# Four TensorE jobs of a decoder step moved into the next chunk, and a new order of the cross-attention jobs in chunk 47

## The reference

```python
h = rmsnorm(x, g_mix)
proj = h @ w_in                      # pool channels | q | k | v, 512 each
A = causal pooling of 4 channel groups, windows 2, 4, 8, 16, then a map per group
B = attention, 8 heads of 64, rotary  # prompt: causal; decode: 256 cached keys + own
x = x + concat(A, B) @ w_out
q = rmsnorm(x, g_cross) @ w_cq       # 4 heads of 256
p = softmax(q . mk / 16)             # 256 memory keys
x = x + (p @ mv) @ w_co
x = x + relu(rmsnorm(x, g_mlp) @ w_up)**2 @ w_down
y = rmsnorm(x, g_final)
```

## Time and profile before

| | us |
|---|---|
| median of 3 runs (lowest, highest) | 419.35 (419.28, 420.08) |
| the profiled execution, its own time | 421.09 |
| its span, first to last instruction | 419.1 |
| TensorE busy in the span | 412.7 (98%) |
| VectorE, ScalarE, GpSimd busy | 253.1, 227.0, 30.9 |

### The profile page before, as it was taken

The page is one execution under the profiler, slowest core; times in us unless marked ns, Lnnn a source line. Parts: engine busy times, 40 slices in busy tenths (PEclk is TensorE's granted clock), DMA queues, the critical chain, the costliest instruction groups (busy, mean ns, idle before and its releaser), DMA issues.

```text
span 419.1 us, 8425 instructions
## 1 busy us (share of the span) xinstructions
PE 412.7 (98%) x3372; PEld 386.7 (92%) x3372; DVE 253.1 (60%) x400; ACT 227.0 (54%) x392; POOL 30.9 (7%) x41
## 2 busy tenths in 40 slices
PE   9999999999999999999999999999999999999995
PEld 9998989986879998948899999999999999999995
DVE  4799989666355784633259777666667534454302
ACT  5876958725454664424267666566565433453313
POOL 1003026000000220000022000000000000010011
PEclk9999999999999999999999999999999999999999
DMA  8999858965988966989527646555565655545002
GB/s 288 384 386 359 283 194 251 349 253 191 404 295 317 386 218 226 370 309 335 218 102 248 205 141 199 185 187 163 184 200 196 196 172 192 183 158 185 2 2 103
DMA packets 37257, 96.60 MB, mean 230 GB/s; under 512 B 4186, under 2 KB 13274, under 8 KB 37082
## 3 DMA queue, kind: packets, MB, share of 16 engines
q1 hardware_dynamic: 35106, 92.24, 63.3%
q10 hardware_dynamic: 2112, 3.82, 2.5%
HBM read 91.73 MB, written 4.54 MB: 230 GB/s over the span
## 4 chain that ended last, share of the span: by engine, by line
PE 89%; DMA 5%; DVE 2%; SPq 1%; issue 1%; ACT 0%; DVEq 0%
PE psum L1104 75%; PE psum L826 4%; DMA raw<-in_w_in 2%; PE psum L1046 2%; PE psum L941 2%; DMA stage<-in_mem_v 2%; PE psum L954 1%; DMA pages<-in_page_table 1%; PE psum L838 1%; PE psum L878 1%; SPq L772 1%; PE psum L887 1%; PE psum L925 1%; PE psum L947 0%; DVE rstd L1586 0%
## 5 line engine op out<-in xcount | busy, mean ns | idle before, releaser
L1392 DVE TENSOR_TENSOR w_lo<-raw,w_hi 128x1024 fp32r<-128x1024 f32 x67 | 82.4, 1239 | 62.2 <-ACT w_hi L1124 62.0
L1124 ACT ACTIVATE w_hi<-raw 128x1024 fp32r<-128x1024 f32 (+1 forms) x73 | 74.0, 1021 | 60.7 <-PE psum L1104 45.4
L1104 PE MATMUL psum<-mix_hi,w_hi 128*128 128x264 f32 (+1 forms) x288 | 82.8, 287 | 0.0
L1104 PE MATMUL psum<-mix_lo,w_hi 128*128 128x264 f32 (+1 forms) x288 | 81.5, 283 | 0.0
L1104 PE MATMUL psum<-mix_hi,w_lo 128*128 128x264 f32 (+1 forms) x288 | 81.5, 283 | 0.0
L1104 PE MATMUL psum<-act_hi,w_hi 128*128 128x264 f32 x232 | 66.3, 286 | 0.0
L1104 PE MATMUL psum<-act_lo,w_hi 128*128 128x264 f32 x232 | 65.6, 283 | 0.0
L1104 PE MATMUL psum<-act_hi,w_lo 128*128 128x264 f32 x232 | 65.4, 282 | 0.0
L1104 PEld LDWEIGHTS psum<-mix_hi,w_hi 128*128 128x128 f32 x288 | 54.3, 188 | 0.9 <-issue 0.8
L1104 PEld LDWEIGHTS psum<-mix_lo,w_hi 128*128 128x128 f32 x288 | 54.3, 189 | 0.1
L1104 PEld LDWEIGHTS psum<-mix_hi,w_lo 128*128 128x128 f32 x288 | 54.3, 189 | 0.0
(11 more groups left out here) (208 smaller groups left out, 813.7 us busy)
## 6 DMA issues: line engine op xcount, KB each, us to landing
raw<-in_w_down SPq DMA_DIRECT2D x20, 512.0 KB, 3.3
raw<-in_w_up SPq DMA_DIRECT2D x18, 512.0 KB, 4.3
raw_more<-in_w_up SPq DMA_DIRECT2D x14, 512.0 KB, 3.7
stage<-in_mem_v SPq DMA_DIRECT2D x12, 512.0 KB, 6.5
raw_more<-in_w_down SPq DMA_DIRECT2D x12, 512.0 KB, 4.2
stage<-in_cache_v SPq DMA_DIRECT2D x16, 256.0 KB, 6.2
keysT<-in_cache_k SPq DMA_DIRECT2D x16, 256.0 KB, 5.0
keysT<-in_mem_k SPq DMA_DIRECT2D x8, 512.0 KB, 6.5
```

The lines of the kernel that those rows point to most:

```text
L1104: mm = pe.matmul(out, a, b, start=first and m == 0, stop=end_ and m == 2)
L1124: return nc.scalar.activation(out, in_, ACT.Copy, scale=scale)
L1392: V.tensor_tensor(lo_of(c), raw_of(c), hi_of(c).bitcast(F32), ALU.subtract).then_inc(w_lo_ready, 1)
```

## The change

The plan of jobs differs in chunk 47 alone. The table `LATER` names four places inside a chunk (chunk, tile); TensorE runs the jobs listed there behind that tile's matmuls. It leaves them out of its walk through `JOBS`. The other engines, the banks and the buffers still go by `JOBS` and `ORDER`, in which those jobs belong to the chunk before: `S` to 8, `P_T` to 14, `c_attn` to 31, `stat c` to 41.

```diff
-    put(47, ("xP_T", 1), ("xP_S", 2), ("xc_O", 0, 0), ("xP_O", 0), ("xS", 1, 0), ("xS", 1, 1), ("xc_O", 0, 1), ("xP_O", 1), ("xc_T", 1), ("xc_attn", 0), ("xP_S", 3), ("xP_T", 2))
+    put(47, ("xP_T", 1), ("xP_S", 2), ("xc_O", 0, 0), ("xP_O", 0), ("xS", 1, 0), ("xS", 1, 1), ("xP_O", 1), ("xc_O", 0, 1), ("xc_T", 1), ("xP_S", 3), ("xc_attn", 0), ("xP_T", 2))
...
 JOBS = plan_jobs()
+LATER = {
+    (9, 1): [('S', 0)],
+    (15, 0): [('P_T', 0), ('P_T', 1), ('P_T', 2)],
+    (32, 1): [('c_attn',)],
+    (42, 0): [('stat', 'c')],
+}
+LATE_JOBS = [j for late in LATER.values() for j in late]
...
                     if last_of_group and x < len(banks_of(g)) - 1:
                         mm.then_inc(bank_full[bank], 1)
+                    for job in LATER.get((c, x), ()):
+                        run(job)
...
                 for job in JOBS[c]:
-                    run(job)
+                    if job not in LATE_JOBS:
+                        run(job)
```

## The result

The change makes the kernel slower. The median of four runs is 423.92 us (423.13 to 424.45) against 419.58 (419.28 to 420.08), a ratio of 1.0100 with a 95% interval from 1.0085 to 1.0115. The forecast of 419.9 with a range of 418.9 to 420.7 was wrong. The profiled execution took 424.45 us, with a span of 422.4 us.

A forecast was written before the change was run, and what follows sets the result against it. TensorE, busy 412.7 of 419.1 us, was taken to bound the kernel. The moves' -0.28 and chunk 47's +0.83 gave +0.55, which with the median of 419.35 made 419.9 us, range 418.9 to 420.7.

The forecast's parts named there:

- So 2.34 us of TensorE's time is in reach.: Waits the change could remove: 0.83 us at the head scores (`kT`), 1.51 at the second cross output's value tile.
- The moves, -0.28: Sum up to chunk 47: -0.83 at the scores, +0.05 at P_T, +0.45 at S 4, +0.05 for leaving a chunk.
- The waits at P_T and S 4: P_T in chunk 15 loses 0.05 (0 to 0.3); S 4 waits 0.45 (0.2 to 0.75) for its bank.
- a tie by the sum: P_T, moved behind one tile of chunk 15, comes at 53.45; the normalised heads it needs finish at 53.43.
- one of the prediction's own signs of being wrong: A wait at P_T over 0.3 us was listed among what would show the forecast wrong.
- The idle time of VectorE for `w_hi`: Before S 4: 0.35 us idle on VectorE, released by chunk 14's end through ScalarE, was to go.
- The held `w_lo`: Before S 4: GpSimd's addition holds VectorE's second `w_lo` about 0.7 us, bank free at 57.5, wait 0.45.
- `c_attn` and `stat c`: Moves into chunks 32 and 42: TensorE waited at neither, so nothing is gained; no new wait expected.
- Chunk 47, +0.83, bounds 0.5 and 1.2: New order removes the 1.51 us tile wait, but chunk 48 waits for xc_attn 0's low part: net cost 0.83.
- the gain of 1.51 at the value tile: Chunk 47: xP_O 1 ahead of xc_O 0 1 covers the tile's landing, so its 1.51 us wait is gone.
- the softmax chain: xP_S 3's softmax precedes xc_attn 0's low part: 3.0 us from xP_S 3's last issue until chunk 48 can start.
- the clock, put at nothing: Before chunk 48: TensorE idle some 2.2 us; the sum held no term for a lower clock.

The follow-up runs named there:

- e10: The kernel before, no edit, profiled a second time: span 417.7 us, chunk 46 to 48 in 23.11 us.
- e11: The kernel before, no edit, profiled a third time: span 417.0 us, chunk 46 to 48 in 22.61 us.
- e1: The kernel before with the four moved jobs alone, chunk 47 in its old order: 419.58 us against 419.93, ratio 0.9987.
- e4: The changed kernel with the four transposes of xP_T 2 done six times to fill the idle time: 421.93 us against 419.93 before, ratio 1.0056.
- e6: The four moves, with chunk 47's list ending xP_T 2, xc_attn 0, xP_S 3: 419.52 us against 419.79 for the kernel before, ratio 0.9998.
- e2: The kernel before with the new order of chunk 47 alone, no moved job: 424.18 us against 419.93, ratio 1.0096.
- e5: The changed kernel, xc_attn 0 back ahead of xP_S 3 on ScalarE and VectorE, TensorE's order kept: 420.08 us against 419.79 before, ratio 1.0005.
- e7: The changed kernel again, no edit, in a second set of runs: 423.48 us against 419.79 for the kernel before, ratio 1.0080.
- e9: The changed kernel with the transposes of xP_T 2 done three times: 422.03 us against 420.12 for the kernel before, ratio 1.0047.

## Why the prediction was wrong

**"So 2.34 us of TensorE's time is in reach."** Wrong in size. Both waits vary from execution to execution. The tile wait was 1.51 in the shown profile and 0 to 0.78 in four others; the scores start 0.95 behind the last matmul in the shown profile and 0.21 to 0.73 in e10 and e11. A normal step is 0.12, so 0.09 to 0.61 was to be had there. The shown profile's own time, 421.09, was 1.74 above the median of 419.35 that the prediction names beside it (1.0 to 1.5 above the medians of later sets), and part of what I read as the kernel's waits was that execution's. The prediction added its terms to the median as if both were the same execution.

**The moves, -0.28.** Not contradicted: e1 is at -0.35 (-1.2 to +0.1), an interval that holds zero. The waits at P_T and S 4 appeared where they were placed in the changed kernel's profile, but they are no fixed price of the moves: e1, e4 and e6 have the moves and show neither, and e2 has no moves and shows 0.5 for `uext`. Chunk 3 to 16 takes 46.84 to 47.67 in the five profiles without moves and 46.72 to 48.02 in the seven with all four. In the changed kernel's profile they cost more than the gain, +0.57 up to chunk 16, since `kT` ended at 34.26 there and not at 33.71, later than in any other profile, and all of VectorE's work behind it with it. Its rows with TensorE's at the same places:

```profile
33.12 1.14 DVE L1488 TENSOR_TENSOR kT<-kT,crossed 128x528 f32<-128x528 f32 x1
...
52.14 1.83 DVE L1579 TENSOR_TENSOR soft<-soft,stats 128x512 f32<-128x512 f32 x2
...
57.94 0.76 DVE L1443 TENSOR_TENSOR uext<-psum,rstd 128x264 f32<-128x264 f32 x2
```

```profile
34.50 1.59 PE L845 MATMUL psum<-kT,qT 32*128 32x128 f32 x32
...
54.11 1.17 PE L885 MATMUL psum<-const,soft 128*128 128x128 f32 x9 [0.37 <-DVE soft L1579]
...
58.50 0.73 PE L845 MATMUL psum<-kT,qT 32*128 32x128 f32 x16 [0.72 <-DVE uext L1443]
```

P_T stood at a tie by the sum (53.45 against 53.43), and 0.5 us of lateness on VectorE became 0.53 of wait, in full; over 0.3 there was one of the prediction's own signs of being wrong. The idle time of VectorE for `w_hi`, which should have gone with an earlier chunk 14, was also still there: in this execution ScalarE waited for the weights' landing, not for TensorE.

```profile
54.42 1.06 ACT L1134 ACTIVATE w_hi<-raw 128x1024 fp32r<-128x1024 f32 x1 [0.80 <-DMA raw<-in_w_ck]
```

The held `w_lo` did not come about. GpSimd's addition starts at 55.86, 0.35 behind the start of the second `w_lo` and not ahead of it, as in the kernel before (55.26 against 54.91), and that `w_lo` takes 1.22. So S 4's wait came from the lateness alone. The term was also summed wrongly: a bank free 0.43 earlier (57.29) and then held for 0.7 is free at 57.99, which gives a wait of 0.9 and not 0.45.

**`c_attn` and `stat c`.** Right: no wait, and 16 to 46 is 106.77 in both kernels.

**Chunk 47, +0.83, bounds 0.5 and 1.2.** The mechanism was right (e5), the size was not. Chunk 46 to 48 takes 25.33 or 25.34 in all five executions with this order. Against the shown profile that is +1.19, since chunk 48 started 3.24 us behind xP_S 3's last issue (191.56 to 194.80) and not 3.0, and xP_S 3 itself came 0.12 later in the frame of chunk 46. The 2.87 up to the end of the scalings were met exactly (191.56 to 194.43); the small low part and the signal took 0.37 and not 0.15. But against the old order as it usually runs (22.61 to 23.41) it is +1.9 to +2.7: the tile wait that the new order takes away is mostly not there. Without that wait the old order needs 22.62 and the new one 2.71 more: 2.44 in front of chunk 48 (2.80 from the last transposes to its start, against 0.36) and 0.27 in the steps before.

**The step that failed, part one: the gain of 1.51 at the value tile,** set against the softmax chain in the term +0.83. It was one execution's wait, 0 to 0.78 in four others, so the term, bounded by 0.5 and 1.2, came out at +1.9 to +2.7.

**Part two: the clock, put at nothing.** The forecast said that TensorE would stand idle for some 2.2 us, and it did, 2.20; nothing in the sum gave that idle time an effect behind its end, and no reason was given. Chunk 48's first matmul to chunk 49's takes 6.88 where the clock fell and 5.31 to 5.43 in all that kept it, 1.56 for each fall. It fell in eleven of sixteen executions, and with the twenty filling transposes in none of six. The Trainium skill (TensorE: Matmul & The Clock Gate, Part 1: The HAM clock gate) describes the two levels, and that the lower one comes after idle time; the trace agrees, with 0.50 granted from 195.8 to 199.2.

**Sum.** Moves -0.3, order +1.9 to +2.7, clock +1.56 for each fall. The four executions of the first comparison all had the fall: +3.2 to +4.0 against +4.3 measured. In e7 half had it: +2.4 to +3.2 against +3.7. In e4 and e9 none had it: +1.6 to +2.4 against +2.0 and +1.9. So 0.3 us or more stay open in the first two, up to 1.3; executions of one kernel differ by more than that (the kernel before in e7's set from 419.08 to 422.97).

## What to carry over

Before pricing the removal of a wait from one profile, look at how that execution stands to the median, and at the same wait in a second profile: a wait for a transfer can be 1.5 us in one and nothing in the next. When a job moves in one engine's list that all engines follow, ask what stands ahead of its last small step on each of the others; here a 0.20 us instruction was put behind a whole softmax. An idle time of TensorE of about two microseconds cost itself here and, in most executions, 1.56 us more in clock: keep it short, or put work in it.

## What was not expected of the hardware

The same idle time of 2.2 us was followed by the 1.2 GHz level in eleven executions of sixteen, and 1.33 us in none of six. The place of the fall differed too: 1.0 us after TensorE was back at work in one trace (195.8, chunk 48 from 194.80), so that the first matmuls ran 0.12 us apart and the later ones 0.22, and 0.03 us after it in the other (e7, 195.13 and 195.10). Both falls lasted 3.41 us and cost 1.56. Twenty transposes that compute nothing new, or eight, made the changed kernel faster by about 2 us.
